# MoE on one core: the load of an expert's down weights moved from SyncE's DMA queue to ACT's

## What is computed

```python
def _hierarchical_moe(x, w_rg, b_rg, w_re, b_re, w_gate, w_up, w_down):
    ...                                # each token: a group, then the top 2 of its 8 experts
    def expert_block(args):
        xb, e = args
        h = jax.nn.silu(xb @ w_gate[e]) * (xb @ w_up[e])
        return h @ w_down[e]

    y_rows = lax.map(expert_block, (x_rows, block_e)).reshape(n_rows, d)
    y = jax.ops.segment_sum(y_rows * row_gate[:, None], row_tok, num_segments=t + 1)[:t]
```

## Time and profile before

| | us |
|---|---|
| median of 3 runs | 5101.12 (5096.52 to 5119.75) |
| the profiled execution | 5109.23 |
| its span | 5107.5 |
| TensorE busy | 4043.2 (79%) |
| ACT busy | 623.5 (12%) |
| queue q1 (SP's), share of the 16 engines over the span | 34.9% |
| queue q10 (ACT's) | 1.5% |

### The profile page before, as it was taken

The page is one execution under the profiler, slowest core; times in us unless marked ns, Lnnn a source line. Parts: engine busy times, 40 slices in busy tenths (PEclk is TensorE's granted clock), DMA queues, the critical chain, the costliest instruction groups (busy, mean ns, idle before and its releaser), DMA issues. The chain is left out here.

```text
span 5107.5 us, 52067 instructions
## 1 busy us (share of the span) xinstructions
PE 4043.2 (79%) x20935; PEld 2472.6 (48%) x20935; DVE 1621.0 (32%) x2870; ACT 623.5 (12%) x1222; POOL 558.9 (11%) x455
## 2 busy tenths in 40 slices
PE   4989969998993866999899547587775988577774
PEld 2578834443462863444348433344433766344442
DVE  6657634302327543000330562200003134300003
ACT  2212110001111221000111100000001023100000
POOL 1123210001002401000100330100001013200001
PEclk9989979999987988999999778799997987699987
DMA  3221216421210002222121002499992200489995
GB/s 117 66 76 52 93 68 209 164 87 57 75 33 0 0 1 79 82 66 94 51 74 50 1 9 74 193 400 402 401 357 92 71 17 1 158 349 398 396 404 227
DMA packets 243069, 707.94 MB, mean 139 GB/s; under 512 B 22140, under 2 KB 117812, under 8 KB 192084
## 3 DMA queue, kind: packets, MB, share of 16 engines
q1 hardware_dynamic: 223172, 662.03, 34.9%
q10 hardware_dynamic: 15120, 26.76, 1.5%
q0 software_dynamic: 4608, 16.78, 0.8%
HBM read 668.28 MB, written 37.24 MB: 138 GB/s over the span
## 5 line engine op out<-in xcount | busy, mean ns | idle before, releaser
L2549 PE MATMUL experts_pg<-moe_wg,experts_xt 128*64 128x256 f32 x4224 | 531.1, 415 | 131.3 <-DMA moe_wg<-in_moe_w_up 112.8
L86 PE MATMUL ffn_in_ps<-ut,ffn_in_ring 128*128 128x512 f32 x1408 | 613.5, 596 | 24.8 <-DMA ffn_in_ring<-in_ffn_w_in 24.8
L2549 PEld LDWEIGHTS experts_pg<-moe_wg,experts_xt 128*64 128x64 f32 x4224 | 333.9, 150 | 311.5 <-issue 161.3
L86 PEld LDWEIGHTS ffn_in_ps<-ut,ffn_in_ring 128*128 128x128 f32 x1408 | 266.7, 190 | 361.9 <-issue 336.3
L465 PE MATMUL ffn_out_y<-ffn_out_ring,ffn_h 128*128 128x512 f32 x704 | 306.7, 598 | 20.0 <-DMA ffn_out_ring<-in_ffn_w_out 20.0
L2564 PE MATMUL experts_py<-moe_wd,experts_ht 128*64 128x512 f32 x1056 | 252.9, 622 | 41.6 <-DVE experts_ht L2616 24.1
L86 PE MATMUL att_proj_ps<-att_proj_ring,ut 128*128 128x512 f32 x576 | 250.2, 597 | 16.7 <-DMA att_proj_ring<-in_attn_w_qkv 16.7
L2614 DVE TENSOR_TENSOR experts_h<-experts_hs,experts_pg 128x256 f32<-128x256 f32 x66 | 27.8, 422 | 651.9 <-ACT experts_hs L2583 651.9
L465 PEld LDWEIGHTS ffn_out_y<-ffn_out_ring,ffn_h 128*128 128x128 f32 x704 | 134.7, 192 | 189.1 <-issue 167.5
L86 PEld LDWEIGHTS att_proj_ps<-att_proj_ring,ut 128*128 128x128 f32 x576 | 177.7, 309 | 88.9 <-DMA att_proj_ring<-in_attn_w_qkv 17.1
L573 DVE TENSOR_TENSOR ffn_h<-ffn_in_act_out,ffn_in_ps 128x512 f32<-128x512 f32 x44 | 30.3, 688 | 531.5 <-ACT ffn_in_act_out L560 531.5
(11 more groups left out here) (623 smaller groups left out, 5694.1 us busy)
## 6 DMA issues: line engine op xcount, KB each, us to landing
moe_wg<-in_moe_w_gate SPq DMA_DIRECT2D x66, 2048.0 KB, 20.2
moe_wg<-in_moe_w_up SPq DMA_DIRECT2D x66, 2048.0 KB, 24.7
moe_wd<-in_moe_w_down SPq DMA_DIRECT2D x66, 2048.0 KB, 25.8
ffn_in_ring<-in_ffn_w_in SPq DMA_DIRECT2D x44, 1024.0 KB, 7.7
ffn_in_ada_ring<-in_ada_w SPq DMA_DIRECT2D x28, 1024.0 KB, 7.3
ffn_out_ring<-in_ffn_w_out SPq DMA_DIRECT2D x22, 1024.0 KB, 5.2
ssd_proj_ring<-in_ssd_w_in SPq DMA_DIRECT2D x20, 1024.0 KB, 5.3
att_proj_ring<-in_attn_w_qkv SPq DMA_DIRECT2D x9, 2048.0 KB, 7.8
```

The source lines that it names most:

```text
L86: last = nc.tensor.matmul(out, lhsT, rhs, start=(i == 0), stop=(i == len(pairs) - 1))
L2549: last = nc.tensor.matmul(pg[ch * SLOTS:(ch + 1) * SLOTS, b, side, 0:HH], xt[:, b, kk % MQ, kk // MQ, :], wg[:, b, side, kk, ch * HH:(ch + ...
```

## The change

The two lines that make SP wait for `y_made` and load the down weights are taken out of `load`. ACT gets four lines at the head of `one`, for all blocks but the first two: it reads the expert from `info`, waits for `y_made` of block n - 2 (the same wait) and issues the same load on its own queue. ACT comes to these lines when it has finished block n - 1: its SiLU, its copy out of PSUM and its two stores. Gate and up weights and the rows of x stay on SP's queue. Buffers, semaphores and all computation are the same.

```diff
@@ SP, load(i, b, first)
                         if not first:
                             sp.wait_ge(s["gu_made"], i - 1)
                             load_gate_up(sp, bass.ds(e, 1), b)
-                            sp.wait_ge(s["y_made"], i - 1)
-                            load_down(sp, bass.ds(e, 1), b)
@@ ACT, one(n, b, it, first)
                     def one(n, b, it, first=False):
+                        if not first:
+                            e = act.value_load(info[0:1, bass.ds(n, 1)], min_val=0, max_val=E - 1)
+                            act.wait_ge(s["y_made"], n - 1)
+                            load_down(act, bass.ds(e, 1), b)
                         act.wait_ge(s["gu_made"], n + 1)
                         if not first:
                             act.wait_ge(s["h_done"], n - 1)
```

## The result

The changed kernel takes 5193.8 us (median of 4 runs, 5185.9 to 5195.6) against 5103.7 us before (5096.5 to 5119.8): ratio 1.0169, 95% interval 1.0142 to 1.0196. The forecast was 5121 us, +0.4%, with a range to 5155. The change costs 90 us, over four times what the sum gave, and the time lies above the range.

The account below looks back on a forecast made before the run. The prediction took the DMA engines to bound the two expert loops. Slow-clock blocks +6, fill +5.4 and drain +5.4 and +2.8 made about +20 us on the 5101.1 us median: 5121 us, range 5095 to 5155.

Parts of the forecast that it names:

- the sum: Both expert loops: slow-clock blocks +6, fill +5.4, drain +5.4 and +2.8, about +20 us together.
- What bounds the loop before: Both expert loops: DMA engines set the pace, 17.0 us a block at 402 GB/s against TensorE's 14.4.
- ACT's own part: ACT, each block: register read, wait and load, issued 2.9 us after the down product; costs nothing, covered until the SiLU.
- the wait that moves to w_down: TensorE, each block: w_down late by 0 to 5 us, replacing the wait before gate/up; alone costs nothing.
- What would show it: List of signs: among them w_down waits of about 2.5 us, some 60 us a loop, and DMA share staying 1.02.
- In steady state nothing runs dry at full clock: Inside the loops: DMA engines always have queued work when the next load arrives, so no loss at full clock.
- margins of 3.1 and 2.7 us: Engines' work left when the next w_down and gate/up loads arrive, counted from g, the end of block n - 1's gate/up.
- The clock term, +6: Blocks with slow gate/up and down groups pass the margin by 0.7 to 1.8 us: 3 us a loop, +6 in two.
- Rival (a): Slower clock after the moved wait: a third of 66 blocks lose 1.5 us, 5148 us; every block, near 5210; chance 0.27.
- Fill and drain, +13.5: Loop edges: idle engines near each start, +5.4 in two loops; later last down products, +5.4 and +2.8.
- (b): Both loops: no loss, a second queue fills gaps, 2% more rate cancels the added time: 5101 us, chance 0.17.
- (c): Both loops: faster, full filling raises the rate from 402 to 420 GB/s: 5074 us, chance 0.06.

Follow-up runs that it names:

- e4: The kernel before with w_up loaded only for blocks 0 and 1, stale weights used afterwards: 4989.6 us.
- e7: The kernel before with the rows of x loaded only for blocks 0 and 1, stale rows used afterwards: 5016.6 us.
- e9_both: The changed kernel with the down load issued ahead of ACT's copy and stores, and six extra matmuls a block before the down product: 5125.3 us, ratio 1.0023.
- the warm kernel: The changed kernel with six extra matmuls a block in the gap before the down product, to keep TensorE busy: 5115.0 us, ratio 0.9986.
- e6_sp_late: The kernel before with the down load one block later, still on SP's queue: 5128.1 us, ratio 1.0019.
- e3: The changed kernel with ACT issuing the next block's down load ahead of its copy and two stores: 5128.1 us, ratio 1.0026.
- e11_after_no_x: The changed kernel with the rows of x loaded only for blocks 0 and 1, stale rows used afterwards: 5129.7 us.
- e1_act_early: The changed kernel with ACT issuing the down loads one block earlier, on its own queue: 5165.2 us, ratio 1.0101 to the kernel before.

## Why the prediction was wrong

**What bounds the loop before**: right. The DMA engines do, and kernels that take nothing but bytes from them, e4 and e7, are 122 and 89 us faster.

**ACT's own part, the issue at product end + 2.9 us, and the wait that moves to w_down**: right in place and nearly in size, 3.3 us on average and a wait of 2.8 us a block. I called the 3 us costless because ACT's SiLU is covered. That looked at the wrong cover. They lie on the chain from one down product to the next, and taking the 3 us out is worth 66 us by the medians (5193.8 to 5128.1) and 73 by the ratios, each against the kernel before of its own series (1.0169 to 1.0026). Of 3 us a block only 1.1 comes back, since the engines then set the pace. The wait itself was under-counted in "What would show it": 2.5 us a block make 75 to 80 us a loop, not 60, and 80.8 and 90.2 were measured.

**"In steady state nothing runs dry at full clock"**: this step failed. I had worked out margins of 3.1 and 2.7 us from a time g, and both were too large. I counted the wait w in full as work for the engines, though w_down shares it with gate/up that were counted already; and I counted the rows of x and the stores as queued, though both are issued only after the product's end (3614.53 and 3614.58 above), when the queues are nearly empty. With w = 4.2 us in the block shown, gate/up's 10.4 us and half of the shared time, the engines have work until about 3602.1 + 0.9 + 10.4 + 2.5 = 3615.9; w_down's packets cannot be there before 3616.85 + 0.9 = 3617.8. The windows show the hole, 260 GB/s from 3614 to 3618. So in this block there was no margin but a gap of about 2 us, and the chain, not the engines' work, set the pace. The time to landing was not the mistake: 12.7 us was worked out for a 2 MB load that shares full engines, and where they stayed full (e9_both) it is 13.3; in the change it is 9.5, because they do not.

**The clock term, +6**: this is the same step's size. I took the present number of slow groups, 5 down products in the first loop, over into a kernel in which the wait had moved right ahead of the down product. There 28 of 31 are slow in the first loop and 28 of 33 in the second, 56 where the kernel before has 7: the granted clock is 0.71 of full speed in the window that holds the down product (3609 to 3614), and a product takes 5.35 us where it takes 3.65 at the higher level. Rival (a) named the mechanism, with 0.27, but gave it too high a point of decision, 2.7 us, since that was the false margin. It also expected slow gate/up groups with it; none is slow in the change behind the first of each loop, where the kernel before has 25. That its "in every block near 5210" lies nearest to the 5193.8 is luck: it took 4.2 us a block less a margin of 2.7, where 1.7 without a margin was lost. The down products are busy 348.2 - 252.9 = 95 us longer, about as much as the loss; the warm kernel gives back 79 by the medians and 93 by the ratios.

It would be wrong to call one of the two the cause. The chain is 3.3 + 9.5 + 5.3, and the loop's pace is the longer of the chain and the engines' 16.6 to 17.0 us. Either remedy brings the chain down to the engines' time or near it, each is worth 66 to 93 us alone, and both together no more (1.0023).

**Fill and drain, +13.5**: plausible and not shown apart. e6_sp_late, with full engines, is 10 to 15 us slower than the kernel before, and e3 and e9 have 0.2 to 0.3% more; but the sum of a late load's costs there includes more than these two. In the change the last block of the first loop takes 14.2 us (down product ends at 3855.4 and 3869.6), as forecast; in the second it is 16.2. The hole of the fill is there as well: from 3316 to 3318 us the DMA share is 0.14, about 2 us of idle engines where 2.7 were forecast. What it costs in a loop that the chain paces no run shows.

**Rivals (b) and (c)**: the hope for rate from a second queue was wrong in sign. On the second queue at full load the rate fell to 384 GB/s, and the slices of 420, which I took for what could be filled, were those without rows of x: without these both kernels run at 422. In the change itself that effect does not make the loss, as e11_after_no_x shows. The Trainium skill's rule that the issuing engine does not make a separate path ("DMA: Bandwidth & Descriptors", "Issuing engines are not separate DMA queues") holds for the weights, 422 against 421 GB/s. Beside the rows of x interleaving cost rate in one kernel, 384 against 402.

What stays open: why rows of x slow the weights beside them. They are the only loads of the loop that write 64 partitions, and the only ones in 2 KB pieces; no run parts these two. That the loss of rate lasts as long as packets of rows are under way is seen; why they are spread so thin in e1_act_early is not tested.

## What to carry to other kernels

A prefetch is worth what it keeps queued: before moving a load, draw the chain from the event that issues it to the event that it releases and back, with issue, landing under load, and the consumer at the clock it will have after a wait, and compare its length with the engines' time for a period. If it is near, microseconds of unrelated work on the issuing engine, here a copy and two stores, cost time until the chain is as short as the engines' period, however idle that engine is: 3 us a block cost 1.1.

If a wait is moved to stand right ahead of a matmul group, price that group at the lower clock, and count the slow groups anew rather than taking over the old number.

## What the runs showed of the hardware that was not expected

The rows of x are 0.26 of the 6.8 MB of a block, 3.8%, but cost 89 us of 1070 (5105.6 to 5016.6), 8%: without them the rate of the weights is 422 instead of 402 GB/s. With the down weights loaded as early on a second queue the rows cost another 46 us (52 with them, 6 without) at a DMA share of 1.02 in both cases, so a full share of busy engines does not say what they move.

Six useless matmuls a block made a kernel 79 us faster, as the granted clock stayed at its higher level in front of the group on the chain (0.96 and 0.99 of full speed in the middle of the two loops, 0.87 and 0.88 without them), and changed nothing where that group was not on it (ratio 0.9992).
